# Doubling the 64x64 inverses in blocks of two chunks: odd heads' products cross the partition halves, ScalarE copies the new inverse, VectorE turns it in four blocks

## What is computed

```python
def _rwkv7_scan(r, w, k, v, kk, b):
    """S_t = S_{t-1} diag(w_t) - (S_{t-1} kk_t)(kk_t*a_t)^T + v_t k_t^T ; y_t = S_t r_t."""
    ...
    def step(state, inp):
        r_t, w_t, k_t, v_t, kk_t, b_t = inp
        sa = jnp.einsum('bhij,bhj->bhi', state, kk_t)
        state = (state * w_t[:, :, None, :]
                 - sa[..., None] * b_t[:, :, None, :]
                 + v_t[..., None] * k_t[:, :, None, :])
        y = jnp.einsum('bhij,bhj->bhi', state, r_t)
        return state, y
```

## Time and profile before

| | |
|---|---|
| median of 3 runs | 1266.04 us |
| lowest and highest | 1265.31 and 1266.44 us |
| span of the profiled execution | 1262.8 us |
| its whole time | not listed; the median lies 3.2 us above the span |
| doubling stage | 184 to 320 us of the span |
| PE busy in the span | 1240.3 us (98%) |
| DVE, ACT, POOL busy | 765.1, 586.2, 398.5 us |
| granted TensorE clock | 0.999 in the mean, no slice of the span under 0.9 |

### The profile page before, as it was taken

One profiled execution on the slowest core, in us unless ns is written; L12 is line 12 of the kernel. 1 busy time (PEld: TensorE's weight loads), 2 busy tenths in 40 slices (PEclk: granted clock), 3 DMA queues, 4 the chain that ended last, 5 costly groups with the idle time before them and its releaser, 6 DMA issues.

```text
span 1262.8 us, 26628 instructions
## 1 busy us (share of the span) xinstructions
PE 1240.3 (98%) x11269; PEld 1142.4 (90%) x11269; DVE 765.1 (61%) x1037; ACT 586.2 (46%) x1036; POOL 398.5 (32%) x314
## 2 busy tenths in 40 slices
PE   8999999999899999999999999999999999999998
PEld 7777798888899999999999997776899999999997
DVE  6678745555558529458377567434584494673863
ACT  5545535445455426337145453545443262461652
POOL 6022236223004236236253233000051362443520
PEclk9999999999999999999999999999999999999999
DMA  6223300000433323323324232112223233232331
GB/s 199 67 67 100 100 2 3 3 4 3 143 126 101 101 67 109 126 72 130 101 73 156 74 108 77 59 67 78 74 76 125 69 101 115 86 111 91 101 118 67
DMA packets 102076, 108.88 MB, mean 86 GB/s; under 512 B 1972, under 2 KB 97254, under 8 KB 101959
## 3 DMA queue, kind: packets, MB, share of 16 engines
q1 hardware_dynamic: 101878, 106.93, 26.9%
q0 software_dynamic: 80, 0.26, 0.1%
HBM read 105.08 MB, written 2.10 MB: 85 GB/s over the span
## 4 chain that ended last, share of the span: by engine, by line
PE 91%; DVE 4%; ACT 2%; issue 1%; POOL 1%; DVEq 0%; POOLq 0%; ACTq 0%
PE ps L556 11%; PE ps L558 11%; PE ps L557 11%; PE ps L647 6%; PE ps L648 6%; PE ps L649 6%; PE ps L520 4%; PE ps L522 4%; PE ps L521 4%; PE ps L607 2%; PE ps L609 2%; PE ps L608 1%; PE ps L1179 1%; PE ps L870 1%; PE ps L1181 1%
## 5 line engine op out<-in xcount | busy, mean ns | idle before, releaser
L556 PE MATMUL ps<-w_hi,a_hi 128*128 128x256 f32 x1024 | 286.1, 279 | 0.0
L557 PE MATMUL ps<-w_lo,a_hi 128*128 128x256 f32 x1024 | 285.8, 279 | 0.0
L558 PE MATMUL ps<-w_hi,a_lo 128*128 128x256 f32 x1024 | 285.8, 279 | 0.0
L556 PEld LDWEIGHTS ps<-w_hi,a_hi 128*128 128x128 f32 x1024 | 192.4, 188 | 0.1
L557 PEld LDWEIGHTS ps<-w_lo,a_hi 128*128 128x128 f32 x1024 | 192.4, 188 | 0.1
L558 PEld LDWEIGHTS ps<-w_hi,a_lo 128*128 128x128 f32 x1024 | 192.4, 188 | 0.0
L1911 DVE TENSOR_TENSOR w_lo<-w_raw,w_hi 128x2048 fp32r<-128x2048 f32 (+1 forms) x55 | 131.0, 2382 | 72.3 <-ACT w_hi L1269 72.0
L1269 ACT ACTIVATE w_hi<-w_raw 128x2048 fp32r<-128x2048 f32 (+1 forms) x55 | 104.4, 1899 | 133.1 <-PE ps L558 108.3
L2834 POOL TENSOR_TENSOR hsq<-tmp 128x512 f32<-128x512 f32 x64 | 94.9, 1498 | 88.9 <-ACT tmp L1381 62.3
L2017 DVE TENSOR_TENSOR w_lo<-w_raw,w_hi 128x1024 fp32r<-128x1024 f32 (+1 forms) x72 | 94.8, 1331 | 26.1 <-ACT w_hi L1342 25.9
L647 PE MATMUL ps<-th,w_hi 128*128 128x256 f32 x384 | 108.0, 281 | 0.4 <-ACT tmp L1367 0.4
(11 more groups left out here) (420 smaller groups left out, 3112.4 us busy)
## 6 DMA issues: line engine op xcount, KB each, us to landing
w_raw<-w_ffn_up_dram SPq DMA_DIRECT2D x16, 1024.0 KB, 5.7
w_raw<-w_ffn_down_dram SPq DMA_DIRECT2D x16, 1024.0 KB, 5.2
w_raw<-w_up_dram SPq DMA_DIRECT2D x16, 1024.0 KB, 5.6
w_raw<-w_down_dram SPq DMA_DIRECT2D x16, 1024.0 KB, 5.2
w_raw<-w_in_first_dram SPq DMA_DIRECT2D x12, 1024.0 KB, 5.3
w_raw<-w_out_dram SPq DMA_DIRECT2D x8, 1024.0 KB, 5.4
xn<-x_dram SPq DMA_DIRECT2D x8, 512.0 KB, 5.1
w_raw<-w_in_dram SPq DMA_DIRECT2D x4, 1024.0 KB, 6.4
```

The source lines that it names most:

```text
L556: mm(o, hi[:, hb + k, tok], whi, start=first and own and k == ks[0], stop=False, skip_group_check=True)
L557: mm(o, hi[:, hb + k, tok], wlo, start=False, stop=False, skip_group_check=True)
L558: m = mm(o, lo[:, hb + k, tok], whi, start=False, stop=last and k == ks[-1], skip_group_check=True)
```

## The change

Level 1 keeps its `double`. Its `update` writes the products of odd heads' tiles into another bank, and from there on the two halves of the tile are kept so that the transposed inverse of (c, e) stands at head group c xor e. From level 2 on, `double` sends e = 1 to the other partition half and `update` sends it back, four (c, e) in turn within each p. `Qm` becomes 1 - Q: one DVE subtraction from the identity over all 8 heads takes the place of the two copies. Since R'(1 - Q) is the new transposed inverse itself, the subtraction L2440 and its counterpart L2446 are gone; ACT copies the result from PSUM to `Tm` (or to `Rm` at level 5), and DVE waits for that copy (`t_ready`) and turns it into `Rm` with four transposes of 64x256, two of them from one partition half to the other. `solve` reads `Rm` with the halves of the head index exchanged. The products write to columns 256 to 511 of the banks in `update` and 0 to 255 in `double`.

```diff
+            straight_then_crossed = ((0, 0), (1, 0), (0, 1), (1, 1))
+
+            def turned_out(c, e, p):
+
+                return ps[half[c], c ^ e, 256 + p * CH:256 + (p + 1) * CH]
+
             def double(i, l):
                 n = nl * i + l
                 pe.wait_ge(sm["m_ready"], n + 1)
                 pe.wait_ge(sm["t_ready"], n + 1)
-                for pair in (same_first[0:2], same_first[2:4]):
+                if l == 0:
+                    for pair in (same_first[0:2], same_first[2:4]):
+                        for p in range(HP):
+                            for c, e in pair:
+                                h = e * HP + p
+                                m = mm(ps[half[c], e, p * CH:(p + 1) * CH], Mt[half[c], n % 2, h, :], Tm[half[c], h, :],
+                                       start=True, stop=True)
+                else:
                     for p in range(HP):
-                        for c, e in pair:
-                            h = e * HP + p
-                            m = mm(ps[half[c], e, p * CH:(p + 1) * CH], Mt[half[c], n % 2, h, :], Tm[half[c], h, :],
-                                   start=True, stop=True)
+                        for c, e in straight_then_crossed:
+                            m = mm(ps[half[c ^ e], c, p * CH:(p + 1) * CH], Mt[half[c], n % 2, e * HP + p, :],
+                                   Tm[half[c], (c ^ e) * HP + p, :], start=True, stop=True)
                 m.then_inc(sm["q_done"], 1)
             def update(i, l):
                 n = nl * i + l
-                pe.wait_ge(sm["q0_ready"], n + 1)
-                pe.wait_ge(sm["q1_ready"], n + 1)
+                pe.wait_ge(sm["q_ready"], n + 1)
                 if l == 0:
                     pe.wait_ge(sm["r0_ready"], i + 1)
+                    after("r_final", i)
+                    for e in range(2):
+                        for p in range(HP):
+                            for c in range(2):
+                                h = e * HP + p
+                                m = mm(turned_out(c, e, p), Rm[i][half[c], h, :], Qm[half[c], h, :], start=True, stop=True)
                 else:
                     pe.wait_ge(sm["r_turned"], (nl - 1) * i + l)
-                for pair in (same_first[0:2], same_first[2:4]):
                     for p in range(HP):
-                        for c, e in pair:
-                            h = e * HP + p
-                            q, rm = Qm[half[c], h, :], Rm[i][half[c], h, :]
-                            o = ps[half[c], e, p * CH:(p + 1) * CH]
+                        for c, e in ((0, 0), (1, 0), (1, 1), (0, 1)):
+                            x, h = half[c ^ e], c * HP + p
+                            q, rm = Qm[x, h, :], Rm[i][x, h, :]
                             if l < nl - 1:
-                                m = mm(o, rm, q, start=True, stop=True)
+                                m = mm(turned_out(c, e, p), rm, q, start=True, stop=True)
                             else:
-                                m = mm(o, q, rm, start=True, stop=True)
+                                m = mm(turned_out(c, e, p), q, rm, start=True, stop=True)
                 m.then_inc(sm["dt_done"], 1)
             def solve(i, b):
...
-                            m = mm(ps[half[c], b + e, p * P:(p + 1) * P], Rm[i][half[c], h, :], KG[i % 2][half[c], h, :],
+                            m = mm(ps[half[c], b + e, p * P:(p + 1) * P], Rm[i][half[c], (c ^ e) * HP + p, :], KG[i % 2][half[c], h, :],
...
                 for l in range(nl):
                     n = nl * i + l
-                    act.wait_ge(sm["q_done"], n + 1)
-                    af(Qm[:, 0:HP, :], ps[:, 0, 0:256].rearrange("q (p t) -> q p t", t=CH), ACT.Copy).then_inc(sm["q0_ready"], 1)
                     beside(i, 2 * l)
                     attend(2 * n)
+                    act.wait_ge(sm["dt_done"], n + 1)
+                    dst, ready = (Tm, "t_ready") if l < nl - 1 else (Rm[i], "r_final")
+                    af(dst[:, :, :].rearrange("q (s p) t -> q s (p t)", s=2), ps[:, 0:2, 256:512], ACT.Copy).then_inc(sm[ready], 1)
                     beside(i, 2 * l + 1)
                     attend(2 * n + 1)
                     if i == 0 and l < HP:
...
                 for l in range(nl):
                     n = nl * i + l
                     dve.wait_ge(sm["q_done"], n + 1)
-                    v.tensor_copy(Qm[:, HP:H, :], ps[:, 1, 0:256].rearrange("q (p t) -> q p t", t=CH)).then_inc(sm["q1_ready"], 1)
+                    v.tensor_tensor(Qm[:, :, :].rearrange("q (s p) t -> q s p t", s=2),
+                                    identc[:, :].unsqueeze(1).unsqueeze(1).broadcast_to([P, 2, HP, CH]),
+                                    ps[:, 0:2, 0:256].rearrange("q s (p t) -> q s p t", t=CH), ALU.subtract).then_inc(sm["q_ready"], 1)
                     beside(i, 2 * l)
                     attend(2 * n)
-                    dve.wait_ge(sm["dt_done"], n + 1)
-                    dt = ps[:, 0:2, 0:256]
                     if l < nl - 1:
-                        t = Tm[:, :, :].rearrange("q (e p) t -> q e (p t)", e=2)
-                        v.tensor_tensor(t, t, dt, ALU.subtract).then_inc(sm["t_ready"], 1)
-                        dve.drain()
-                        v.transpose(Rm[i][:, :, :].rearrange("q h t -> q (h t)"), Tm[:, :, :].rearrange("q h t -> q (h t)"))\
-                            .then_inc(sm["r_turned"], 1)
-                    else:
-                        r = Rm[i][:, :, :].rearrange("q (e p) t -> q e (p t)", e=2)
-                        v.tensor_tensor(r, r, dt, ALU.subtract).then_inc(sm["r_final"], 1)
+                        dve.wait_ge(sm["t_ready"], n + 2)
+                        for c, e in ((0, 0), (1, 0), (0, 1), (1, 1)):
+                            src, dst = slice(c * CH, (c + 1) * CH), slice((c ^ e) * CH, ((c ^ e) + 1) * CH)
+                            m = v.transpose(Rm[i][dst, c * HP:(c + 1) * HP, :].rearrange("q p t -> q (p t)"),
+                                            Tm[src, (c ^ e) * HP:((c ^ e) + 1) * HP, :].rearrange("q p t -> q (p t)"))
+                        m.then_inc(sm["r_turned"], 1)
                     beside(i, 2 * l + 1)
```

More of the change, by code:

```diff
@@ L239, in program @@
             "v_turned", "v_ready", "kap_turned", "kap_ready", "kt_turned", "kt_ready", "bt_turned", "bt_ready",
-            "gv_done", "gv_ready", "r0_ready", "t_ready", "m_ready", "q_done", "q0_ready", "q1_ready", "dt_done",
+            "gv_done", "gv_ready", "r0_ready", "t_ready", "m_ready", "q_done", "q_ready", "dt_done",
             "r_turned", "r_final", "wu_done", "wu_ready", "f_done", "f_ready", "yt_done", "yt_ready", "x_done", "s_ready",
```

## The result

The changed kernel takes 1278.74 us (median of 4 runs, 1275.40 to 1280.96), the kernel before 1265.82 us beside it. The ratio is 1.0101, 95% interval 1.0084 to 1.0118. I had forecast 1266.1 us, no change, and a range up to 1271.5. The kernel got slower instead, and by more than the range allows.

The account below looks back on a forecast made before the run. The stage looked PE-bound, but DVE's queue behind the new inverse was level with PE in many places, so PE's 15.5 us gain would go in waits on DVE and ACT; terms summed to +0.1, giving 1266.1 us, range 1261 to 1271.5.

Parts of the forecast that it names:

- What TensorE gains: `double` and `update`, levels 2 to 5: crossing saves 0.48 us in each of 32 groups, 15.5 us of PE's time.
- PE-led levels: Level 2 of blocks 1, 2 and 3, level 4 of block 1: each gains 0.96 us, together -3.8.
- (a): ACT's copy of 128x512 from PSUM, between `update` and the next `double`: 0.60 us, replacing DVE's subtraction of 0.69.
- (b): DVE's subtraction from the identity, 128x512 with PSUM, between `double` and `update`: 0.69 us, taken from 0.65 to 0.75.
- Rival 4: Crossed products don't run together here, so no 0.48 us saving anywhere: 1274 us, chance 0.06.
- (c): DVE's transpose of 64x256: 0.45 us, four overlapping at 0.37 to 0.38, 1.48 us until the next instruction.
- rival 3: The four blocks on DVE don't overlap, 0.45 us a block, +3.5: 1269.7 us, slower, chance 0.14.
- Levels led by VectorE, +0.27 to +0.36: Levels where PE waits behind DVE's transposes: +0.27 us each in the basic case, +0.36 in level 5 of blocks 1 and 2.
- the sum's +0.1: All level terms and the way out added over the stage: +0.1 us, from rounding -0.4 to +0.4.
- the credit for the earlier inverse: Per level, from `update`'s start to the inverse ready: 1.33 us instead of 1.90, a gain of 0.57.
- The way out, +0.4: Block 3, from the last inverse to `solve`: 5.95 us instead of 5.55, +0.4.
- Rivals 1 and 2: 1: transposes cheap, 0.27 to 0.31 us a block, 1261 to 1263.5, chance 0.17; 2: PE-bound throughout, 1250.6 us, chance 0.05.

Follow-up runs that it names:

- one turn and two blocks: Changed kernel, VectorE's maximum and beside moved ahead, block 3's turned keys first, four blocks replaced by one 128x512 transpose plus two crossed blocks: 1258.39 us.
- products two at a time: Changed kernel with the 32 products of each crossing group reordered to run two at a time instead of four: 1278.44 us.
- half by half: Kernel before with its turn as four 64x256 blocks in place, both of the lower 64 partitions first, then both upper: 1275.25 us.
- the filled kernels: Changed kernel with constant-tile transposes added in TensorE's waits: 1277.74 us with some waits filled, 1271.35 us with more filled and split w_lo moved ahead.
- split ahead: Kernel of one turn and two blocks with VectorE's split w_lo moved ahead of the last advance of the state: 1256.51 us, ratio 0.9927.
- all long waits filled: Changed kernel with 8 constant-tile transposes in ten levels, 12 ahead of the turned-keys wait, and split w_lo ahead of the last advance: 1271.35 us.

## Why the prediction was wrong, step by step

- **What TensorE gains**: right. A crossing group is busy 0.69 us at full clock, like L912, where it was 1.15, and what follows starts 0.52 to 0.63 us behind its start where nothing waits. The stage's own busy time fell by 14.2 us, but that window now holds 116 fewer matmul instructions and part of it is at half clock. A profile at full clock throughout says it better: with one turn and two blocks PE is busy 1226.1 us of the span against 1240.3, 14.2 less, where 15.5 was forecast.
- **PE-led levels**: right. From `double` to `double` level 2 of blocks 1, 2 and 3 got 0.88, 0.91 and 0.99 us shorter and level 4 of block 1 0.63, forecast 0.96 each: -3.4 where -3.8 stood.
- **Durations (a), (b)**: right, 0.59 and 0.685 us. Rival 4 fell by the 0.69 us of a crossing group: its products run together.
- **The turn, (c)**: this step failed. Length 0.44 as forecast, but no overlap: 1.83 us to the next instruction instead of 1.48. The 0.07 us were read in the earlier trace rows from operations that all start at partition 0, and the row I put against rival 3 (two masks in 1.25 us) has the same start too. The blocks change it every time. The rows were right and didn't bear on the case. Rival 3 was thus the true mechanism of this term, with 0.14 to its name. Its 1269.7 us lies close to about 1270.2 for after at clock 0.999 (span 1268.5 and 1.7 around it), but that is in part luck, since it priced only the overlap and the next term was mis-sized as well.
- **Levels led by VectorE, +0.27 to +0.36**: mis-sized beyond the overlap. 11 levels x 0.35 are 3.9 us, and with the sum's +0.1 that makes 4.0 of the 5.7 or so lost at equal clock. From `double` to `double` in the profiled runs, where no stretch at half clock lies in the level: level 3 of blocks 0 to 3 +0.42, +0.45, +0.48 and +0.72 us (forecast +0.27, -0.15, -0.15, +0.27), level 4 of blocks 2 and 3 +0.64 and +1.23 (+0.27, +0.8), level 5 of block 2 +1.68 (+0.36), and level 5 of block 0 -0.37, where I had +0.84. So single terms miss both ways. Of the largest of these, 1.3 us in level 5 of block 2, 0.35 are the overlap and 0.57 the credit for the earlier inverse, which I gave every level. Block 2, level 5, at full clock:

```profile
285.69 1.80 DVE L2458 STREAM_TRANSPOSE Rm<-hsq 64x256 f32<-64x256 f32 x4 [1.32 <-ACT hsq L1759]
...
286.51 0.69 PE L862 MATMUL ps<-hsq,tmp 64*64 64x64 f32 x32
287.52 1.29 DVE L2321 TENSOR_TENSOR LA<-ps,tri 128x512 f32<-128x512 f32 x2
...
288.86 1.10 PE L800 MATMUL ps<-krkv 64*64 64x128 f32 x32 [1.66 <-DVE LA L2321]
```

  `double` starts 0.8 us after the blocks do, because TensorE had the weights' and values' products in front of it, so the earlier inverse gained it nothing. From `double` to L800 it is 2.35 us. Before it was 1.21:

```profile
281.33 1.15 PE L850 MATMUL ps<-hsq,tmp 64*64 64x64 f32 x32
...
282.54 1.10 PE L800 MATMUL ps<-krkv 64*64 64x128 f32 x32
```

- **No term for the clock**: this was the largest miss, about 7 us. The forecast named the waits on negmax, the masks and Yt, and said PE's idle time would go up by some 15 us. It treated idle time as free wherever the level's sum came out even. Waits of 1.3 to 1.9 us, where there had been none over 0.7 up to the solve, are a change of kind.
- **The way out, +0.4**: measured +0.78 from level 5's `double` to the solve (322.01 to 328.13 against 314.19 to 319.53), and then 2.3 us more behind the solve, of which at most 1.7 are the half clock from 328.7 to 332.1 us. I had put that stretch at nothing.
- **Rivals 1 and 2**: fell as cases of this kernel. (Rival 1's 4.8 us at 0.27 a block should read 4.4 by its own 0.44 us a step.) But part of TensorE's gain was there to be had: with VectorE's queue out of the way the same products, copy and blocks give 0.9938, and with one turn and two blocks, the keys and the split moved ahead, 0.9927.

## What to carry over

When a step on an engine gets longer, list what is queued behind it on that engine and who waits for each; if none of it needs the step, move it ahead. Here that turned +1.0% into -0.6% with every operation kept. Read an overlap of two operations only from rows whose operands start at the same partitions as the new ones. Give waits of 1.4 us and more on TensorE a price of their own. And compare runs by span at equal mean clock before a difference is put down to an edit, since two medians (after and "products two at a time") were equal while the kernels were some 4 us apart.

## What the runs showed of the hardware

**Start partition and overlap on VectorE.** With unchanged start partitions the next operation starts 0.07 to 0.08 us before the end of the one before (128x256, and 64x256 in the order half by half); with a change it starts 0.01 to 0.03 us behind the end. That holds for an operation of 128 partitions behind a block that started at 64, too. The Trainium skill, "VectorE: DVE Perf Modes", section "Two Vector instructions with no wait between them", has this as a model: an instruction whose input or output starts in another quadrant of 32 partitions than the last one's in the same memory is held until all earlier ones have finished. Every spacing of the turns here agrees. The order in which blocks (row half to row half) are written can't avoid it in the changed kernel, since of its four blocks each differs from the next in the half it reads or the half it writes. The same page's "Terms" entry on DRAIN, which I had cited for rival 3, says that no next operation may start before the pipe is empty; the starts 0.08 us ahead of the end speak against it in that general form.

**The clock.** TensorE's granted clock fell to 1.2 GHz behind waits of 1.5 to 1.9 us: at 192.2, 205.8, 250.2 and 328.7 us in after, with 1.7 us of clock lost each time. The waits ended at 191.6, 203.8, 248.9 and 328.1. In all profiled runs there are 16 such stretches up to 1250 us, all between 184 and 360, in 8 kernels, and each began between 0.9 us before and 2.0 us after the end of a wait of TensorE of 1.37 to 1.94 us. Not every such wait did it: of 38 waits of that length between 184 and 360 us 22 were followed by full clock, among them 1.66, 1.77 and 1.69 us, ended at 288.9, 310.5 and 317.2, in after itself. Runs of one kernel differ in how often it happens (mean clock 0.988 to 0.994). The Trainium skill, "TensorE: Matmul & The Clock Gate", Part 1, describes a gate that halves the clock depending on how busy TensorE has just been; the filled kernels agree with that. What length of wait is safe stays open here: the kernels whose longest waits in and just behind the stage were 1.34 us (split ahead) and 1.03 (all long waits filled) kept 0.999 to 1.000 in all eight runs, and before, with one of 1.69 us, did not.
